# Seams of a hybrid transformer layer: values in 16 transfers, a merge that begins with attention's branch, output weights split inside the merge, and turns of the identity at block ends

## The reference

```
hx = modulate(rmsnorm(x));  zx = hx @ w_in + b_in          # also k, v of the context tokens
hy_x = hyena_mixer(zx[:, :1536])                            # long convolutions by FFT, gated, 512 wide
na_x = neighbourhood_attention(q, k, v, context k and v)    # 8 heads of 64, grid of width 64, 512 wide
mix  = (sigmoid(g_hy) * (hy_x @ w_branch_hy) + sigmoid(g_na) * (na_x @ w_branch_na)) @ w_out
x    = x + g1 * mix
x    = x + g2 * expert_choice_moe(modulate(rmsnorm(x)))     # 16 experts, 128 tokens each, SwiGLU, 2816 wide
out  = rmsnorm(x)
```

## Time and profile before

| what | us |
|---|---|
| median of 3 runs (lowest, highest) | 2703.47 (2702.67, 2703.78) |
| the profiled execution's time | 2703.3 |
| its span (first to last instruction) | 2700.7 |
| norm_and_project | 0 to 359.1, values loaded until 373 |
| attend | 373.1 to 534.6 |
| hyena | 538.0 to 886.9 |
| merge | 887.2 to 985.5 |
| project_out | 985.8 to 1109.0 |
| choose | 1109.8 to 1150.2 |
| experts | 1150.5 to 2700.7 |

### The profile page before, as it was taken

How to read it: one execution, slowest core, us unless ns; L and a number is a source line. 1 busy time by engine, 2 the same in 40 slices (tenths; PEclk the granted TensorE clock), 3 DMA queues, 4 the chain that set the end, 5 groups by cost and what they waited for, 6 DMA issues and landing times.

```text
span 2700.7 us, 32209 instructions
## 1 busy us (share of the span) xinstructions
PE 2545.6 (94%) x12577; PEld 2121.3 (79%) x12577; DVE 2121.3 (79%) x1976; ACT 1469.9 (54%) x1249; POOL 149.3 (6%) x159
## 2 busy tenths in 40 slices
PE   6999979999999899389999999999999999999997
PEld 2777869878878778368888888888888888888885
DVE  5674247667879555688888888889888888888887
ACT  4522136531121222177777777777777777777774
POOL 0011000011111000000000000000000000000000
PEclk9999989999999999689999999999999999999998
DMA  7498774464566733399999999999999999999994
GB/s 272 161 314 306 248 228 111 135 200 140 162 200 197 236 104 131 155 339 362 386 390 373 374 392 381 363 383 394 370 373 392 380 366 383 389 375 367 392 382 171
DMA packets 198628, 794.93 MB, mean 294 GB/s; under 512 B 17935, under 2 KB 65399, under 8 KB 128528
## 3 DMA queue, kind: packets, MB, share of 16 engines
q1 hardware_dynamic: 168196, 704.75, 69.4%
q0 software_dynamic: 30128, 88.11, 10.6%
q10 hardware_dynamic: 158, 0.07, 0.0%
HBM read 723.38 MB, written 69.48 MB: 294 GB/s over the span
## 4 chain that ended last, share of the span: by engine, by line
PE 53%; ACT 2%; issue 2%; DVE 1%; DVEq 0%; ACTq 0%
PE moe_ps_gate L2210 18%; PE moe_ps_up L2210 16%; PE moe_ps_y L2200 16%; PE moe_ps_h L2181 2%; ACT moe_w_hi L2251 1%; PE moe_ps_x L2173 1%; DVE raw L2373 0%; ACT moe_xt_hi L2244 0%; DVE moe_w_lo L2303 0%; DVE moe_h L2324 0%; ACT moe_sl L2264 0%; DVE raw L2360 0%; PE moe_ps_gate L2234 0%; PE moe_ps_gate L2236 0%; PE moe_ps_up L2234 0%
## 5 line engine op out<-in xcount | busy, mean ns | idle before, releaser
L2303 DVE TENSOR_TENSOR moe_w_lo<-raw,moe_w_hi 128x2048 fp32r<-128x2048 f32 x528 | 1207.6, 2290 | 159.8 <-ACT moe_w_hi L2251 159.6
L2251 ACT ACTIVATE moe_w_hi<-raw 128x2048 fp32r<-128x2048 f32 x528 | 1011.0, 1919 | 379.2 <-PE moe_ps_gate L2210 128.4
L2210 PE MATMUL moe_ps_up<-moe_w_hi,moe_xt_hi 128*128 128x512 f32 (+1 forms) x768 | 292.4, 381 | 0.0
L2210 PE MATMUL moe_ps_gate<-moe_w_hi,moe_xt_hi 128*128 128x512 f32 (+1 forms) x768 | 289.1, 376 | 1.4 <-DVE moe_xt_lo L2294 1.4
L2210 PE MATMUL moe_ps_gate<-moe_w_hi,moe_xt_lo 128*128 128x512 f32 (+1 forms) x768 | 286.5, 373 | 0.0
L2210 PE MATMUL moe_ps_up<-moe_w_hi,moe_xt_lo 128*128 128x512 f32 (+1 forms) x768 | 286.4, 373 | 0.0
L2210 PE MATMUL moe_ps_gate<-moe_w_lo,moe_xt_hi 128*128 128x512 f32 (+1 forms) x768 | 286.1, 373 | 0.0
L2210 PE MATMUL moe_ps_up<-moe_w_lo,moe_xt_hi 128*128 128x512 f32 (+1 forms) x768 | 285.9, 372 | 0.0
L2200 PE MATMUL moe_ps_y<-moe_w_hi,moe_ht_hi 128*128 128x512 f32 x704 | 218.5, 392 | 0.0
L2200 PE MATMUL moe_ps_y<-moe_w_hi,moe_ht_lo 128*128 128x512 f32 x704 | 217.0, 389 | 0.0
L2200 PE MATMUL moe_ps_y<-moe_w_lo,moe_ht_hi 128*128 128x512 f32 x704 | 217.0, 389 | 0.0
(11 more groups left out here) (278 smaller groups left out, 3707.1 us busy)
## 6 DMA issues: line engine op xcount, KB each, us to landing
raw<-in_w_moe SPq DMA_DIRECT2D x528, 1024.0 KB, 7.2
hyena_g_parts<-gw_d POOLq DMA_DIRECT2D x64, 512.0 KB, 4.7
proj_w_mod<-in_w_mod SPq DMA_DIRECT2D x32, 512.0 KB, 7.3
gw_d<-proj_g_parts POOLq DMA_DIRECT2D x16, 1024.0 KB, 7.4
w_in<-in_w_in SPq DMA_DIRECT2D x12, 1024.0 KB, 7.6
attn_table<-in_na_table SPq DMA_DIRECT2D x16, 576.0 KB, 5.6
norm_w_mod<-in_w_mod SPq DMA_DIRECT2D x16, 512.0 KB, 7.1
proj_g_raw<-in_w_in SPq DMA_DIRECT2D x16, 512.0 KB, 9.5
```

Of the source, the lines that this page charges most:

```text
L2210: mm = pe.matmul(ps, hp[:, e % 2, k, :], wp[:, r, :], start=(k == 0 and x == 0), stop=(k == KD - 1 and x == 2))
L2251: act.activation(w_hi[:, g % PARTS], raw[:, g % RAW], ACT.Copy).then_inc(hi_ready, 1)
L2303: dve.tensor_tensor(w_lo[:, g % PARTS], raw[:, g % RAW], w_hi[:, g % PARTS].bitcast(F32), ALU.subtract).then_inc(lo_ready, 1)
```

## The change

It touches five places.

1. load_values: a block of 128 partitions comes by one transfer, whose source has three levels: 4 rows of the grid, 32 tokens, 512 values. 64 transfers of 64 KB become 16 of 256 KB; the counts in product's wait follow.
2. hyena: in the last pass SP, between two stores of gates, issues the loads of the first branch weights (two of 256 KB) and of three of the four tiles of na (512 KB each); ACT splits the weights and a tile of na (the other three at its end), DVE makes the lo halves of the weights and of that tile between the transforms and the outputs. PE ends with 18 turns (FILL) of the identity.
3. merge: block d = 0 begins with attention's branch, and y is split meanwhile. For d = 3 to 6, ACT and DVE split one tile of w_out each (k = 0 to 3); before the last gating DVE splits the first tile of tokens (split_tokens). PE ends with 18 turns of the identity, into the bank of d = 6.
4. project_out: only k = 4 to 7 are split there, and no first tile of tokens. The tiles get places that are free earlier.
5. experts: PE starts with 36 turns of the identity (WARM); the second half of the first expert's tokens is turned into ps_h, without a wait for the first; unit 0 waits for the first half alone and unit 1 for both; DVE makes xt_lo behind two units' splits instead of three and ahead of three small operations.

The core of the diff (tile places, names and semaphores left out):

```diff
-def load_values(sp, a, keep, kg):
+def load_values(eng, a, keep, kg):
     for b in range(4):
-        for r in range(4):
-            first = (4 * kg + r) * GRID_W + BAND_AT[b]
-            sp.dma_start(keep["v_band"][BAND * r:BAND * (r + 1), v_block(kg, b), 0:HEADS * HD],
-                         a["v_d"][first:first + BAND]).then_inc(keep["v_in"][kg // 3], 16)
+        first = 4 * kg * GRID_W + BAND_AT[b]
+        rows = bass.AP(a["v_d"].tensor, first * HEADS * HD, [[GRID_W * HEADS * HD, 4], [HEADS * HD, BAND], [1, HEADS * HD]])
+        eng.dma_start(keep["v_band"][:, v_block(kg, b), 0:HEADS * HD], rows).then_inc(keep["v_in"][kg // 3], 16)
...
-pe.wait_ge(v_in[g], 16 * 48 if g == 0 else 16 * 16)
+pe.wait_ge(v_in[g], 16 * 12 if g == 0 else 16 * 4)
...
+if p == PASSES - 1 and r == 1:
+    sp.wait_ge(tap_used, PH * PASSES)
+    sp.wait_ge(a_done, a_at["seg", p, PH - 1] + 1)
+    for b, w in enumerate(branch_sources(a)):
+        sp.dma_start(coming["b_raw"][:, 0, b], w[0]).then_inc(branch_in[0], 16)
+    for k in range(NA_SLOTS):
+        load_na(k)
...
+load_na(NA_SLOTS)
...
+pe.wait_ge(a_used, len(a_order))
+for _ in range(FILL):
+    pe.transpose(ps_a[:, 0, 0:P], ident[:], ident[:])
...
+if p == PASSES - 1:
+    act.wait_ge(branch_in[0], 32)
+    act.activation(coming["b_hi"][:, 0], coming["b_raw"][:, 0], ACT.Copy).then_inc(bh_ready, 1)
+    act.wait_ge(out_done, NB * p)
+    high_na(0)
...
+for k in range(1, 4):
+    high_na(k)
...
+dve.wait_ge(bh_ready, 1)
+dve.tensor_tensor(coming["b_lo"][:, 0], coming["b_raw"][:, 0], coming["b_hi"][:, 0].bitcast(F32),
+                  ALU.subtract).then_inc(bl_ready, 1)
+low_na(dve, coming, 0)
...
+def low_na(dve, at, k):
+    dve.wait_ge(at["in_hi_ready"], k + 1)
+    dve.tensor_tensor(at["lo"][1][:, k], at["na_raw"][:, k % NA_SLOTS], at["hi"][1][:, k].bitcast(F32), ALU.subtract
+                      ).then_inc(at["in_lo_ready"], 1)
...
+pe.wait_ge(in_lo_ready, k + 1 if b else 4 + k + 1)
...
-branch(0, 0, 0, first=True)
-branch(0, 1, 0)
+branch(0, 0, 1, first=True)
+branch(0, 1, 1)
 for th in range(2):
-    branch(0, th, 1, first=not th).then_inc(branched, 1)
+    branch(0, th, 0, first=not th).then_inc(branched, 1)
...
+pe.wait_ge(merged, 2 * KD + 1)
+for _ in range(FILL):
+    pe.transpose(ps[:, 0, 0, 0:P], keep["ident"][:], keep["ident"][:])
...
+for k in range(4):
+    act.activation(in_hi[0][:, k, :], y_t[:, k, :], ACT.Copy).then_inc(in_hi_ready, 1)
+for d in range(1, KD):
+    split(d % 2, d // 2, d)
+    if d == OUT_FROM:
+        act.wait_ge(in_lo_ready, 8)
+    if d >= OUT_FROM and d - OUT_FROM < 4:
+        k = d - OUT_FROM
+        act.wait_ge(keep["wo_in"][0], 32)
+        act.activation(keep["out_w_hi"][0][:, k, :], keep["wo_raw"][:, k, :], ACT.Copy
+                       ).then_inc(keep["wo_hi"], 1)
...
+for k in range(1, 4):
+    low_na(dve, at, k)
+for k in range(4):
+    dve.wait_ge(in_hi_ready, 4 + k + 1)
+    dve.tensor_tensor(in_lo[0][:, k, :], y_t[:, k, :], in_hi[0][:, k, :].bitcast(F32),
+                      ALU.subtract).then_inc(in_lo_ready, 1)
+
+for d in range(KD):
+    if d + 1 < KD:
+        split(d + 1, (d + 1) % 2)
+    gated(d, 0)
+    if d == KD - 1:
+        dve.wait_ge(merged, 4 + 2 * d + 1)
+        split_tokens(dve, dt, keep, m_t, 0, 0)
+    gated(d, 1)
+    if d >= OUT_FROM and d - OUT_FROM < 4:
+        low_out(dve, keep, d - OUT_FROM)
...
+OUT_FROM = 3
+FILL = 18
...
+def split_tokens(dve, dt, keep, m_t, t, s):
+    src = m_t[:, :, bass.ds(t * P, P)] if not isinstance(t, int) else m_t[:, :, t * P:(t + 1) * P]
+    hi, lo = keep["out_m_hi"][s], keep["out_m_lo"][s]
+    dt.then_wait(dve.tensor_scalar(hi[:], src, 1.0, None, ALU.mult))
+    dve.tensor_tensor(lo[:], src, hi[:].bitcast(F32), ALU.subtract).then_inc(keep["m_split"], 1)
+
+
+def low_out(dve, keep, k):
+    dve.wait_ge(keep["wo_hi"], k + 1)
+    dve.tensor_tensor(keep["out_w_lo"][k // 4][:, k % 4, :], keep["wo_raw"][:, k, :],
+                      keep["out_w_hi"][k // 4][:, k % 4, :].bitcast(F32), ALU.subtract).then_inc(keep["wo_lo"], 1)
...
+act.wait_ge(wo_in[1], 32)
+for k in range(4, KD):
+    act.activation(w_hi[1][:, k - 4, :], w_raw[:, k, :], ACT.Copy).then_inc(wo_hi, 1)
...
-split(0, 0)
-for k in range(KD):
-    dve.wait_ge(wo_hi, k + 1)
-    dve.tensor_tensor(w_lo[:, k, :], w_raw[:, k, :], w_hi[:, k, :].bitcast(F32), ALU.subtract
-                      ).then_inc(wo_lo, 1)
+for k in range(4, KD):
+    low_out(dve, keep, k)
...
+WARM = 36
...
+def x_turned(e, half):
+
+    return ps_h if (e, half) == (0, 1) else ps_x
...
-if half or e:
+if e:
...
+else:
+    pe.wait_ge(x_parts, 2)
...
+for n in range(WARM):
+    pe.transpose(ps_x[:, n % 4 * P:(n % 4 + 1) * P], ident[:], ident[:])
...
-pe.wait_ge(x_parts, 2 * e + 2)
+if e:
+    pe.wait_ge(x_parts, 2 * e + 2)
 for u in range(N_U):
+    if e == 0 and u < 2:
+        pe.wait_ge(x_parts, u + 1)
...
-for g in range(AHEAD):
+split(0)
+split(1)
+for half in range(2):
+    low_x(0, half)
+for g in range(2, AHEAD):
...
-low_x(0, 0)
-low_x(0, 1)
```

More of the change, by code:

```diff
@@ L1203, in hyena @@
         decay_in, gate_in, v2_in = keep["w_mod_in"][0:3]
+        coming = keep["merge"]
+        branch_in, na_in, na_hi_ready, na_lo_ready, bh_ready, bl_ready = (
+            coming[n] for n in ("w_in", "na_in", "in_hi_ready", "in_lo_ready", "bh_ready", "bl_ready"))
         LOADED = 16 * MOD_CHUNKS
@@ L1607, in _, with merge_places, branch_sources @@
                         transform(U_LEAF[q], U_SPEC[q], nothing)
+NA_SLOTS = 3
+def merge_places(nc, sems):
+    with ExitStack() as ctx:
+        m = Maker(nc, ctx, "merge_")
+        at = {"b_raw": m.sb("b_raw", [P, 2, 2, 4, P]),
+              "b_hi": m.sb("b_hi", [P, 2, 2, 4, P], F32R), "b_lo": m.sb("b_lo", [P, 2, 2, 4, P], F32R)}
+        m.sb("room", [P, PH * 2 * P])
+        at["na_raw"] = m.sb("na_raw", [P, NA_SLOTS, T])
+        hi, lo = [None, None], [None, None]
+        hi[0], hi[1] = m.sb("y_hi", [P, 4, T], F32R), m.sb("na_hi", [P, 4, T], F32R)
+        at["gate"] = m.sb("gate", [P, 2, 2, T])
+        lo[0], lo[1] = m.sb("y_lo", [P, 4, T], F32R), m.sb("na_lo", [P, 4, T], F32R)
+        at["hi"], at["lo"] = hi, lo
+    at["w_in"] = [sems(f"branch_in{s}") for s in range(2)]
+    for n in ("na_in", "in_hi_ready", "in_lo_ready", "bh_ready", "bl_ready"):
+        at[n] = sems(n)
+    return at
+def low_na(dve, at, k):
+    dve.wait_ge(at["in_hi_ready"], k + 1)
+    dve.tensor_tensor(at["lo"][1][:, k], at["na_raw"][:, k % NA_SLOTS], at["hi"][1][:, k].bitcast(F32), ALU.subtract
+                      ).then_inc(at["in_lo_ready"], 1)
+def branch_sources(a):
+    return [a[n].rearrange("(k p) (d c) -> d p k c", p=P, c=P) for n in ("w_branch_hy", "w_branch_na")]
 def merge(nc, sems, a, keep, y_t, m_t):
@@ L1685, in split @@
                     act.activation(b_hi[:, s], b_raw[:, s], ACT.Copy).then_inc(bh_ready, 1)
-                for b, src in enumerate((y_t, na_t)):
-                    if b:
-                        split(0, 0, 0)
-                        act.wait_ge(na_in, 64)
-                    for k in range(4):
-                        act.activation(in_hi[:, b, k, :], src[:, k, :], ACT.Copy).then_inc(in_hi_ready, 1)
-                with act.Fori(0, KD // 2 - 1) as i:
-                    split(1, i, 2 * i + 1)
-                    split(0, i + 1, 2 * i + 2)
-                split(1, KD // 2 - 1, KD - 1)
+                for k in range(4):
[9 more added lines that the diff above has]
+                                       ).then_inc(keep["wo_hi"], 1)
             @block.vector
@@ L1735, in _, with gated @@
-                split(KD - 1, 1)
-                gated(KD // 2 - 1, 0)
-                gated(KD // 2 - 1, 1)
+                def gated(d, th):
+                    s = d % 2
+                    cols = slice(th * 512, (th + 1) * 512)
+                    dve.wait_ge(branched, 4 + 2 * d + th + 1)
+                    dve.wait_ge(g_in[s], 32 * (d // 2) + 32)
+                    for b in range(2):
+                        dt.inc(dve.tensor_tensor(gate[:, s, b, cols], ps[:, 2 * s + th, b, :], gate[:, s, b, cols], ALU.mult))
+                    dt.wait()
+                    dve.tensor_tensor(m_t[:, d, cols], gate[:, s, 0, cols], gate[:, s, 1, cols], ALU.add
+                                      ).then_inc(merged, 1)
@@ new lines, with out_places @@
+OUT_FROM = 3
+FILL = 18
+def out_places(nc):
+    with ExitStack() as ctx:
+        m = Maker(nc, ctx, "out_")
+        at = {n: [None, None] for n in ("out_w_hi", "out_w_lo", "out_m_hi", "out_m_lo")}
+        for name, half in (("w_hi", 0), ("m_lo", 0), ("w_hi", 1), ("m_lo", 1), ("w_lo", 0), ("m_hi", 0), ("w_lo", 1), ("m_hi", 1)):
+            at["out_" + name][half] = m.sb(f"{name}{half}", [P, 4, D] if name[0] == "w" else [P, KD, P], F32R)
+    return at
+def split_tokens(dve, dt, keep, m_t, t, s):
[3 more added lines that the diff above has]
+    dve.tensor_tensor(lo[:], src, hi[:].bitcast(F32), ALU.subtract).then_inc(keep["m_split"], 1)
```

(6 more changed lines are left out.)

91 lines of the change are left out of this document (33 added, 58 removed).

## The result

The changed kernel takes 2708.34 us in the median of 20 runs (2705.10 to 2714.38). The kernel before, run 20 times beside it, takes 2701.71 (2698.13 to 2707.81). The ratio is 1.0027, with a 95% interval from 1.0020 to 1.0033: **slower by 0.27%**, where 2692 was forecast, and outside the range. The profiled execution of the changed kernel has a span of 2706.1 us and a time of 2707.91.

The account below looks back on a forecast made before the run. Expert matmuls took over half of the chain that ended last; only waits at seams between stages could go. 2703.3 + 5.8 (attention) - 10.4 (merge, output projection) - 6.2 (experts) = 2692.5, given as 2692; 8-in-10 range 2683 to 2702.

Parts of the forecast that it names:

- values: first product: Attention: twelve value loads, each on four engines at 2.56 us, bring the first product at 385.7 instead of 381.92, 3.8 later.
- values: end of attention: Attention ends 5.8 us later: 3.8 for the first product, 2.0 for restarting at 1.2 GHz, 0 for further waits.
- merge and output projection: Seams behind Hyena and merge: -6.9 for the merge and -3.5 for the output projection, -10.4 us together.
- experts: Start of experts: unit 0 begins 3.9 us earlier and its first matmuls at 2.4 GHz save 2.3; -6.2 us.
- Four engines: Value loads: source's outermost count of 4 puts each 256 KB load on four engines; part of the main sum, chance 0.60.
- count of 52 packets without data: ACT queue, seven loads: one such packet per engine used, so engines divide the row count; sixteen engines would need 112.
- 0 to 4 us of further waits, I take 0: Attention behind the first product: last four value loads, second table and next head come at the pace they are wanted.
- slow-engine rival: Value loads: four engines at 17.3 GB/s each, first product 18.6 us late, some 4 to 6 more behind; 2712 us, chance 0.08.
- bound of sixteen engines: Value loads use all sixteen engines: attention begins at 361.3, gaining 12.0 us and 0.7 of clock; 2674 us, chance 0.10.
- The clock's 2.0 and 2.3: Starts of merge and output projection: us saved if identity turns hold PE at 2.4 GHz instead of 1.2.
- rival of late g_d stores: Hyena's last pass: g_d stores run late behind the five moved loads, +4 us in Hyena; 2696 us, chance 0.08.
- turns' rival: Identity turns don't raise the clock; merge, projection and experts start at 1.2 GHz: +2.0, +2.3, +4.4; 2701 us, chance 0.14.

Follow-up runs that it names:

- run 20: Not a label but part of "run 20 times": the kernel before, unchanged, measured 20 times beside the changed kernel; median 2701.71 us.
- late_table: Changed kernel, but SP waits until the last four value loads have landed before issuing the second head's table, q and k; 2709.9 us.
- wide_values: Changed kernel with the 32 columns outermost in the 16 value loads' source, keys and table reordered to match; 2686.69 us, ratio 0.9943 to the kernel before.
- queues_sp_store_early: Changed kernel with the 64 old value loads, 24 issued by ACT, last two value stores by SP, first expert product two weight splits earlier; 2679.97 us, ratio 0.9920.
- queues_no_turns: Changed kernel with old value loads on SP and ACT, last two value stores by SP, earlier first expert product, no identity turns; 2677.49 us, ratio 0.9912.
- wide_no_turns: Changed kernel with 32 columns outermost in the value loads' source and no identity turns (FILL and WARM 0); 2685.57 us, ratio 0.9942 to the kernel before.
- new_values_only: Kernel before with the 16 new value loads and nothing else changed; 2722.86 us, ratio 1.0069 to the kernel before.

## Why the prediction was wrong, step by step

```
step                                   forecast   measured by the marks
values: first product                    +3.8        +3.9
values: end of attention                 +5.8       +19.3
merge and output projection             -10.4       -10.3   (19.3 to 9.0)
experts                                  -6.2        -2.2   (9.0 to 6.8)
sum                                     -10.8        +6.8
```

**Four engines: right.** The count of 52 packets without data was the right clue, and the working that led to 385.7 for the first product met 384.74 (27.0 and 27.2 us behind the projection's last matmul).

**"0 to 4 us of further waits, I take 0": the step that failed.** The last four loads were taken to be "wanted at the pace at which they come", so at 2.56 us each, in step with the products. They came at 4.3, because the table and the next head's q and k run beside them from 384.5 on; late_table shows that without this company there is no wait. That is 6.6 us at the fifth product. The stop brings two more costs: waits behind the table and the keys (1.81 on DVE, 2.62 on ACT, 3.58 on PE), which the prediction had named only as what would make it wrong, and further falls of the clock, which it had not named. Together the stretch behind the first product lost 15.4 us where 2.0 stood in the sum: 1.2 by the second product, which is the slow restart that the 2.0 was meant for, 6.6 at the fifth, and 7.6 behind it. Holding the table back doesn't make it 0 either: in late_table the fifth product is 5.0 us late and attention ends 14.3 us late, because the table comes late in place of the values. The slow-engine rival came near the time (2712) by a wrong road: it slowed the twelve first loads, which ran at 24.5 GB/s an engine (98 on four), and gave the last four 4 to 6 us of waits. Its closeness is luck.

**The bound of sixteen engines was wrong too.** It let attention begin at 361.3, 1.2 us behind POOL's store. wide_values shows 367.3: the block's end waits 6.1 us in POOL behind its last store. With 6.0 for this, 2.4 for what attention gives back there and 4.0 for the experts (below), the rival's 2674 becomes 2686.4; wide_values measured 2686.69. The sum is made afterwards, and part of this hit is luck: it starts from 2703.3, while the kernel before had a median of 2700.51 beside wide_values.

**Merge and output projection: right**, in the sum. Of its parts, the merge gained 6.4 at its first matmul (-6.0 forecast) and 7.0 by its last (-6.9); project_out gained 2.8 (-3.5). The clock's 2.0 and 2.3 were credited to the turns; without them the merge kept its clock in one trace and lost it for some 3 us in another, and at project_out they were worth 0.56 us in one pair of traces, while in the other the stage was 2.3 faster without them. The second output tile waited 1.93 us, 1.7 by the working. The rival of late g_d stores happened on ACT and not on PE: its wait for the store behind the five loads was 9.28 us where its neighbours are 5.0, and Hyena ended no later (-0.4 by the marks).

**Experts: the start right, the follow-up missed.** Unit 0 gained 4.2 us (-3.9 forecast), and the clock was up. What the step did not ask is who feeds PE next. In DVE's list the changed order puts the lo half of the tokens ahead of the third split, so eight splits instead of seven, 2.28 us more, stand between tokens and first product. DVE is busy without a gap from 1166 to 1186: PE's earlier start ends in a wait of 2.80 us, and the clock that had been saved is lost behind it. By the sixth turn the gain had shrunk from 4.2 to 2.2 us, where 6.2 stood in the sum.

**The turns' rival** said that turns don't count for the clock. On the mechanism it is refuted: in the changed kernel the granted clock was 0.50 from 1158.4 to 1163.3 and 1.00 from 1163.4 to 1164.9, while PE ran nothing but turns, and unit 0 behind them has matmuls of 0.39 to 0.50 us; without turns it begins with 0.79. The Trainium skill (TensorE: Matmul & The Clock Gate, "Part 4: PE-mode transpose") says that the full clock does not engage for transposes; here, in fp32 turns by the identity, the trace doesn't agree. In time, though, the turns were worth nothing, as under this rival, for another reason: in the experts, the stage that they warm is bound by DVE at that point. In the two pairs of traces they were worth 0.0 and 0.8 us from the merge's first matmul to project_out's, and 0.6 and -2.3 from there to project_out's first turn: no gain that both show.

## What to carry to other kernels

Count the engines of a transfer from the outermost level of both of its sides before merging small transfers into large ones; fewer issues are no gain if each then runs on a quarter of the engines. Where a narrow transfer and wide ones meet, price the narrow one at the pace it has beside them, and follow every late landing to the next step that wants it. When a seam is shortened, ask which engine has to have its next result ready, and check that it isn't already busy without a gap.

## What the runs showed of the hardware that was not expected

- A four-engine load of 256 KB took about 2.6 us alone and about 4.3 beside sixteen-wide loads, while all engines together moved 204 to 208 GB/s at a share of 1; in the earlier trace rows the sixteen moved 409. Each value packet took about twice as long as alone (162 and 199 ns, not 87); what it waits for is not settled.
- The drain that POOL runs at this block's end was over 2.1 to 2.2 us after the landing of POOL's last store in each of four traces (before, changed, wide_values, queues_sp_store_early). With a store just issued it took 6.1 us; with the last stores on SP it was through before the block's end.
- A fall of the clock came behind waits of PE of 2.80 us in the experts, 2.98 in project_out, 2.44 at the merge (queues_no_turns) and 2.08 at the second output tile (queues_sp_store_early). It stayed up over 2.38 us at the merge (wide_no_turns), 1.93 at the second output tile (changed kernel), and 1.66 and 1.95 in the experts. The length of one wait doesn't settle it.
- The price of the loads that were moved under Hyena is not settled: Hyena's length was 345.8 us with the loads where they were (new_values_only), 346.9 in the kernel before, and 346.5 to 348.7 in the kernels that moved them.
